# Head norms of an attention stage: sums of squares from two rounded parts instead of one float32 product

## What is computed

```python
def rms_norm(x, g):
    xf = x.astype(jnp.float32)
    y = xf * lax.rsqrt(jnp.mean(xf * xf, axis=-1, keepdims=True) + EPS)
    return (y * g.astype(jnp.float32)).astype(x.dtype)

q, k, v, g, fl = jnp.split(proj, ...)          # 16 heads of 64
q = rms_norm(hd(q), qnorm_g).transpose(0, 2, 1, 3)
k = rms_norm(hd(k), knorm_g).transpose(0, 2, 1, 3)
for blk in range(s_ // FOX_BLOCK):             # 4 blocks of 128 queries
    logits = q[block] @ k[:q1].T * scale + cumf[:, None] - cumf[None, :]
    probs = softmax(where(mask, logits, -inf))
    outs.append(probs @ v[:, :, :q1])
o = o * jax.nn.silu(g)
```

## Time and profile before

| | |
|---|---|
| median of three runs | 2725.76 us |
| the profiled execution | 2727.36 us |
| its span in the trace | 2725.9 us |
| mean granted TensorE clock | 0.996 of full |
| TensorE busy | 2663.0 us, 98% |
| VectorE busy | 1941.1 us, 71% |
| ScalarE busy | 1064.7 us, 39% |
| GpSimd busy | 575.8 us, 21% |

### The profile page before, as it was taken

How to read it: one execution, slowest core, us unless ns; L and a number is a source line. 1 busy time by engine, 2 the same in 40 slices (tenths; PEclk the granted TensorE clock), 3 DMA queues, 4 the chain that set the end, 5 groups by cost and what they waited for, 6 DMA issues and landing times.

```text
span 2725.9 us, 38343 instructions
## 1 busy us (share of the span) xinstructions
PE 2663.0 (98%) x15829; PEld 2294.1 (84%) x15829; DVE 1941.1 (71%) x2645; ACT 1064.7 (39%) x1512; POOL 575.8 (21%) x366
## 2 busy tenths in 40 slices
PE   9899999999999999999999999999999999999998
PEld 6687877678899988878899988999978778788997
DVE  7888644656888865458888788888744743888887
ACT  4444555543443325443333424433322222343342
POOL 2211000101444300002444214443000000044440
PEclk9999999999999999999999999999999999999999
DMA  9453222222333232222333323333423213233331
GB/s 299 143 152 113 62 62 62 78 62 78 109 93 109 94 109 86 70 62 78 109 111 106 109 78 109 96 106 95 134 81 105 86 63 99 62 109 94 97 120 47
DMA packets 297457, 268.31 MB, mean 98 GB/s; under 512 B 10999, under 2 KB 265217, under 8 KB 297026
## 3 DMA queue, kind: packets, MB, share of 16 engines
q1 hardware_dynamic: 294050, 256.99, 30.6%
q0 software_dynamic: 2368, 6.64, 0.7%
q10 hardware_dynamic: 864, 2.23, 0.3%
HBM read 263.72 MB, written 2.10 MB: 98 GB/s over the span
## 4 chain that ended last, share of the span: by engine, by line
PE 76%; DVE 16%; ACT 3%; issue 3%; POOL 1%; DMA 1%; SPq 0%; DVEq 0%; ACTq 0%; POOLq 0%
PE psum L355 13%; PE psum L357 13%; PE psum L356 13%; PE psum L434 6%; PE psum L435 6%; PE psum L436 6%; PE psum L411 2%; PE psum L413 2%; PE psum L412 2%; DVE acc L530 2%; DVE w_lo L340 1%; PE psum L3409 1%; DVE w_lo L1043 1%; DVE stat L679 1%; PE psum L2953 1%
## 5 line engine op out<-in xcount | busy, mean ns | idle before, releaser
L355 PE MATMUL psum<-h_hi,w_hi 128*128 128x256 f32 (+1 forms) x2224 | 721.7, 325 | 18.5 <-DVE f_cffn L1063 6.5
L357 PE MATMUL psum<-h_hi,w_lo 128*128 128x256 f32 (+1 forms) x2224 | 702.8, 316 | 0.0
L356 PE MATMUL psum<-h_lo,w_hi 128*128 128x256 f32 (+1 forms) x2224 | 701.9, 316 | 0.0
L355 PEld LDWEIGHTS psum<-h_hi,w_hi 128*128 128x128 f32 x2224 | 426.0, 192 | 54.0 <-issue 12.7
L356 PEld LDWEIGHTS psum<-h_lo,w_hi 128*128 128x128 f32 x2224 | 426.3, 192 | 29.0 <-issue 5.5
L357 PEld LDWEIGHTS psum<-h_hi,w_lo 128*128 128x128 f32 x2224 | 425.8, 191 | 27.1
L989 POOL TENSOR_TENSOR val<-w_raw 128x512 f32<-128x512 f32 x72 | 100.2, 1392 | 1355.6 <-DMA w_raw<-in_ffn_w_in 954.8
L340 DVE TENSOR_TENSOR w_lo<-w_raw,w_hi 128x2048 fp32r<-128x2048 f32 x98 | 223.4, 2291 | 150.3 <-ACT w_hi L335 140.7
L530 DVE SCALAR_TENSOR_TENSOR acc<-psum,acc 128x512 f32<-128x512 f32 x416 | 269.8, 679 | 42.0 <-PE psum L436 42.0
L355 PE MATMUL psum<-t_hiffn,w_hi 128*128 128x256 f32 x864 | 245.2, 284 | 3.4 <-DVE w_lo L1043 2.3
L356 PE MATMUL psum<-t_loffn,w_hi 128*128 128x256 f32 x864 | 244.5, 283 | 0.0
(11 more groups left out here) (442 smaller groups left out, 5479.9 us busy)
## 6 DMA issues: line engine op xcount, KB each, us to landing
w_raw<-in_ffn_w_in SPq DMA_DIRECT2D x176, 512.0 KB, 5.1
w_raw<-in_ffn_w_out SPq DMA_DIRECT2D x88, 512.0 KB, 6.3
w_raw<-in_ret_w_in SPq DMA_DIRECT2D x48, 512.0 KB, 4.7
ada_raw<-in_ada_w SPq DMA_DIRECT2D x32, 512.0 KB, 4.7
w_raw<-in_odd_w_in SPq DMA_DIRECT2D x32, 512.0 KB, 5.0
w_raw<-in_even_w_in SPq DMA_DIRECT2D x24, 512.0 KB, 6.7
w_raw<-in_gla_w_in SPq DMA_DIRECT2D x24, 512.0 KB, 4.9
ada_first<-in_ada_w SPq DMA_DIRECT2D x32, 256.0 KB, 6.3
```

What stands on the lines that cost most here:

```text
L355: k.nc.tensor.matmul(out, ws, xs, start=first, stop=False)
L356: k.nc.tensor.matmul(out, ws, xl, start=False, stop=False)
L357: return k.nc.tensor.matmul(out, wl, xs, start=False, stop=last)
```

## The change

Each square is made in two float32r parts. ScalarE's square (L2488) writes a rounded `o_sq_hi`. GpSimd makes the exact square from the copied tile and subtracts the rounded one, giving `o_sq_lo`. TensorE multiplies both by a float32r block of ones, so one float32 product becomes two float32r products. In the fills the sum stands two steps later (`m == 5`); the output fill's place is unchanged. At the stage's start the sums move too: k 0 0 from behind `tensor_narrow` to the second step of v, q 0 1 from step 4 to step 6 of v's first half, k 0 1 from step 1 to step 3 of its second half. VectorE's norm also waits for `o_sq_lo`, since it overwrites the copied tile. GpSimd's gates stand between and behind the squares. `o_g` moves into the constants `reset128` and `reset64`, to make room.

```diff
-                if m == 3 and normed:
+                if m == 5 and normed:
                     tensor_head_norm(k, *normed, 7)
...
-    pe.matmul(k.bank[b][:], k.const("block_ones"), k.o_sq, start=True, stop=True
-              ).then_inc(*k.up("o_sum", (w, i, c)))
+    pe.wait_ge(*k.at("o_sq_lo", (w, i, c)))
+    pe.matmul(k.bank[b][:], k.o_ones[:], k.o_sq_hi[:], start=True, stop=False)
+    pe.matmul(k.bank[b][:], k.o_ones[:], k.o_sq_lo[:], start=False, stop=True).then_inc(*k.up("o_sum", (w, i, c)))
...
-    sc.activation(k.o_sq, k.bank[b][:], ACT.Square).then_inc(*k.up("o_sq", (w, i, c)))
+    sc.activation(k.o_sq_hi[:], k.bank[b][:], ACT.Square).then_inc(*k.up("o_sq", (w, i, c)))
+
+
+def gpsimd_square(k, w, i, c):
+
+    po, before = k.nc.gpsimd, norm_before(w, i, c)
+    raw = (k.o_qn if w == "q" else k.o_kn)[:, c, :]
+    po.wait_ge(*k.at("o_raw", (w, i, c)))
+    if before:
+        po.wait_ge(*k.at("o_sq_lo", before))
+    po.tensor_tensor(k.o_sq, raw, raw, MULT).then_inc(*k.pool.up())
+    po.wait_ge(*k.pool.at())
+    po.wait_ge(*k.at("o_sq", (w, i, c)))
+    po.tensor_tensor(k.o_sq_lo[:], k.o_sq, k.o_sq_hi[:].bitcast(F32), SUB).then_inc(*k.up("o_sq_lo", (w, i, c)))
...
     ve.wait_ge(*k.at("o_rs", (w, i, c)))
+    ve.wait_ge(*k.at("o_sq_lo", (w, i, c)))
...
     tensor_narrow(k, S, 2)
-    tensor_head_norm(k, "k", 0, 0, 3)
     pe.wait_ge(*k.at("w_lo", n_v))
-    for x, norms in enumerate(({4: ("q", 0, 1)}, {1: ("k", 0, 1)})):
+    for x, norms in enumerate(({1: ("k", 0, 0), 6: ("q", 0, 1)}, {3: ("k", 0, 1)})):
...
+    sc.activation(k.o_ones[:], k.const("block_ones"), ACT.Copy)
     sc.wait_ge(*k.at("used", AT[S, "q", 0]))
...
 def gpsimd_odd(k):
-    for i in range(4):
-        gpsimd_gate(k, AT["odd", "out", i])
+    for x, (w, i, c) in enumerate(NORMS):
+        gpsimd_square(k, w, i, c)
+        if x == 9:
+            gpsimd_gate(k, AT["odd", "out", 0])
+        if x == 11:
+            gpsimd_gate(k, AT["odd", "out", 1])
+    gpsimd_gate(k, AT["odd", "out", 2])
+    gpsimd_gate(k, AT["odd", "out", 3])
```

More of the change, by code:

```diff
@@ L186 @@
 SAME = ("cross", "cross_copied", "diag", "keep", "out", "values", "cum", "ex", "E", "edge", "q", "sq", "sum",
-        "v_copied", "silu", "S", "turned", "scores", "norm", "half")
+        "v_copied", "silu", "S", "d", "turned", "scores", "norm", "half")
 def signal(name):
@@ L2772, in scalar_fill @@
             sc.wait_ge(*k.at("o_g_raw", (i, 1)))
-            sc.activation(k.o_g[:], k.o_g[:], ACT.Silu).then_inc(*k.up("o_silu", i))
+            sc.activation(k.o_g, k.o_g, ACT.Silu).then_inc(*k.up("o_silu", i))
             sc.preload_act_table_set(EXP_LN)
@@ L3629, in tiles @@
             k.gq8 = sb("o_gq8", [P, 1], ctx=c2)
-            k.o_qn, k.o_kn, k.o_g = (sb(n, [P, 2, T], ctx=c2) for n in ("o_qn", "o_kn", "o_g"))
+            k.o_qn, k.o_kn = (sb(n, [P, 2, T], ctx=c2) for n in ("o_qn", "o_kn"))
+            k.o_g = k.const("reset128", 0, 2 * T).rearrange("p (a n) -> p a n", n=T)
+            k.o_sq_hi, k.o_sq_lo = (sb(n, [P, T], F32R, c2) for n in ("o_sq_hi", "o_sq_lo"))
+            k.o_ones = sb("o_ones", [P, P], F32R, c2)
             k.o_v = [sb(n, [P, NT, 256], ctx=c2) for n in ("o_v0", "o_v1")]
```

## The result

| | before | after |
|---|---|---|
| median of 19 runs each, same comparison | 2726.26 us | 2729.83 us |
| ratio, 95% interval | | 1.0014, [1.0008, 1.002] |
| the profiled execution | 2727.36 us | 2733.22 us |
| its span | 2725.9 us | 2731.7 us |
| mean granted TensorE clock | 0.996 | 0.995 |

The change made the kernel slower by 3.6 us, 0.14%. The interval doesn't contain 1, so the slowing is measured; its amount lies within the 0.2% that the prediction called the same. One of the 19 runs before took 6913.14 us, and the ratio leaves it out. The forecast was +7.6.

What follows compares the result with a forecast made beforehand. The prediction took the stage to be PE's program laid end to end. Its terms, +3.2 - 0.2 + 0.8 + 3.8, gave +7.6 us (6.2 saved against 13.8 in waits), a median of 2733.4 us, range 2725.0 to 2738.

Steps and rivals of the forecast that it cites:

- the likeliest case: Whole kernel: waits outweigh the saved products, +7.6 us, time 2731.3 to 2737; chance 0.52.
- few collisions: Rival: DVE's pairs go through together, POOL's operations fall into DVE's idle time; -0.8 to +5 us, 2725 to 2731; chance 0.35.
- the wait for turned part 4: Product with v, slots 0, 1, 2, 3 and 5: ACT's turned part 4 stands behind the root; 0.6 us each.
- The product: Each norm's sum: two float32r products cost 0.47 us against 0.855 for float32; 0.385 saved, 6.2 us over 16 norms.
- GpSimd's part: From the copy's end to `o_sq_lo`: product and difference take 2.6 us, 2.7 with hand-overs.
- Start: Stage start until the scores of tile 1 in slot 0: waits and DVE collisions, 0.6 to 3.9 us later, taken as +3.2.
- all with them: Upper end at the stage's start: scores of tile 1 start at 353.6 with all collisions, 350.3 without.
- Slots 0 to 4: Eight norms save 3.1 us, turned part 4 costs 2.4, gate 0 costs 0.5: -0.2; slot 4 nothing.
- Slot 5: Late low part, scalings of tile 3 held by POOL and the wait for turned part 4: +0.8 us; -0.7 without collisions.
- Slot 6: Gates 2 and 3 behind k 3 1's difference hold both scalings of tile 0; scores of tile 2 wait 3.8 us.
- As dear as float32: Rival: a float32r pair costs as much as the float32 product, 6.2 us not saved, about 2739; chance 0.05.
- Faster: Rival: products count and waits at the start fill later slack, -5.5 to -6.8 us, 2719 to 2720; chance 0.08.

Runs made afterwards that it cites:

- GpSimd's part made, but not waited for: Kernel after with sums at the old places reading the rounded square twice, nothing on PE or DVE waiting for the low part: 2726.07 us, ratio 0.9997.
- the gates alone: Kernel without GpSimd squares (two products of the rounded square, old places), with each gate put behind the square where the change put it: 2721.43 us, ratio 0.998.
- the third gate moved: Kernel after with the gate of output piece 2 put in front of the square of q 3 1, in slot 5: 2728.16 us, ratio 1.0006.
- the start in float32: Kernel after with the first four norms as in the kernel before (float32 product, no GpSimd square, old places): 2727.93 us, ratio 1.0005.
- the products alone: Kernel after without GpSimd squares, both float32r products reading the rounded square, sums and gates as in the kernel before: 2720.02 us, ratio 0.9976.
- the version with these two mended, and the start left in float32: Kernel after with the first four norms in float32, sums behind the fifth step (sixth in slot 5), gate 2 in slot 5: 2722.13 us, ratio 0.9987.
- the three parts: Separate kernels' effects on the stage: products exchanged -6.0 us, sums' places moved +2.7, GpSimd's work beside VectorE without being waited for +6.1.

## Why the prediction was right and wrong

The range held the time, and the sign of the likeliest case was right. The size was not: +7.6 was forecast, 3.6 came, and the time fell into the 2725 to 2731 of the case called few collisions. I had given 0.35 to within 0.2% and 0.57 to slower by more. The mechanisms of the likeliest case were all there, though: the wait for turned part 4, waits on GpSimd at the start, DVE operations held by gates in slot 6. It was their prices in PE's time that were too high, always in the same direction. So the sign and the range were earned, but the 2729.83 itself was that of a case which I had held to be the less likely.

**The product: right.** 0.385 a norm was forecast, 0.40 came at the places that the earlier trace rows shows, 6.0 us in all when alone.

**GpSimd's part: right, a little long.** 2.6 us was forecast for both operations; 1.04 and 1.28 came. Whether the product is shorter for its one input or for being a product, no run here tells. POOL's busy time rose by 44.5 us, against 42, but 16 norms of 2.32 are 37: the rest is for the most part time in which DVE held GpSimd's operations, which the working had only at the stage's start.

**Start: +3.2 forecast, +1.96 measured.** The wait at the sum of q 0 1 was right: 2.0 to 3.5 forecast, 3.07 came, and the order by which it was worked out (scan, product, k's norm, difference) is nearly that of the trace; only the norm came ahead of the product and not behind it. The step that failed is the last one, "all with them". The wait at k 0 1 was 0.98 and not 1.1 to 1.6, and then nothing was late at the scores of tile 1: PE is there at 354.41 without a wait. DVE was late, its maximum of tile 0 by 3.2 us on the stage's own scale (352.80 against 346.81 us, less the 2.78). But before the change the exponentials behind that maximum were done 1.4 us before PE asked for them (DVE's reciprocal, which waits for them, begins at 348.30, the scores of tile 1 at 349.67), and now PE itself came 2 us later: 0.1 us of slack was left (354.30 against 354.41). 3.07 + 0.98, less four savings of 0.40 and the 0.6 of the earlier trace rows that went, is 1.85. So PE's waits and DVE's delays ran side by side, and this term was the waits on PE alone; DVE's delays alone, with no wait for the low part, cost 3.0 us here (GpSimd's part made, but not waited for). I had put the second behind the first.

**Slots 0 to 4: -0.2 forecast, -0.40 measured.** The wait for turned part 4 was forecast at 0.6 and came at 0.64, five times. The fourth fill's sum took its 0.3 to 0.5 of slack and no more, as forecast. Gate 0 met a scaling, as forecast (456.37 to 460.10 us), and cost PE nothing: the 0.5 put on it was the part that missed. In the kernel with the gates alone the same gate met the negation instead, and there it cost the half microsecond.

**Slot 5: +0.8 forecast, -0.56 measured,** k 3 1's saving in both. The wait for q 3 0's low part was 0.57 against 0.9, and turn 0 waited 0.74 where it was forecast to be 1.3 late. The scalings of tile 3 did have GpSimd's product between them, but it held the second one for 0.8 us (1.66 for the pair against 0.88 in the earlier trace rows), not for a whole product of 1.3. And a wait that was there before became shorter: that for the exponentials before the scores of tile 2 fell from 0.94 to 0.28, since the gate of piece 1 began 0.25 us behind the pair of scalings and let it through. With the third gate moved it began 0.06 behind them, and the wait was 0.9 again, as it was with the start in float32. That part, 0.66 of the 1.4 us by which this term missed, is chance: nothing in the change sets where that gate falls to a fifth of a microsecond, since it starts when its piece is loaded.

**Slot 6: +3.8 forecast, 2.2 measured,** 1.51 and 0.56 in waits. Right: both gates in one row behind k 3 1's difference, two DVE instructions held for almost a gate each. Wrong: which ones. The forecast had both scalings of a pair; the first gate held a negation of 128x2 numbers, which I had not counted as an operation that a gate could hold. And k 3 1's difference ended 2.8 us behind the product with v and not 3.65, so the gate began 0.86 us ahead of the negation (557.05 against 557.91); by the forecast's time it would have begun beside it. That moved the wait from tile 2 to tile 1 and made two small ones of it, and what both hold up overlaps. PE's own arrival was put at 11.7 us on that scale, where the earlier trace rows give 12.27 less 0.385, so 11.9; that slip is 0.2 of the 1.6.

The four terms sum to +3.2 against +7.6, and the misses are 1.2, 0.2, 1.4 and 1.6. Two of the large ones, the start and slot 6, are of one kind: DVE's delays were carried through to PE without the slack between the two, or laid end to end with a delay that ran beside them. The third, slot 5, is half chance. The clock is a price that the prediction put at nothing without a word: at the wait of 3.07 us it fell to 0.50 in two of the three profiles that have this wait, for 0.8 us net, and not in the profile after. The earlier trace rows gave DVE 20 idle us of 31 in a slot, and I used this for the rival only.

What was to be seen if each step held was there: the spacing of 0.23, some 42 us more of POOL, five idle times of 0.6 at the product with v, 2 to 3.5 at the sum of q 0 1. Only the last sign, two scalings of over 4 us in slot 6 and 3.8 in front of tile 2, came in another form.

**The rivals.** "As dear as float32" is ruled out by the products alone. "Faster" was wrong for the change, and right for its parts: it decides where I had put it, at the wait for turned part 4 and at the gates, and the version with these two mended, and the start left in float32, is 3.5 to 4.2 us faster than before. The ports: the Trainium skill ("SBUF — State Buffer", section "SBUF: two separate sides") has the lock for DVE's two-port modes as well as for two SBUF inputs; the cast (0.41 to 1.41) and the 128x2 negation (0.17 to 3.76) bear that out, neither of which has two tiles as input. Maxima, which read PSUM (0.42 at 557.45 us, with a gate under way), were not held. Nor was the reciprocal of 128x2, from SBUF to SBUF (0.17 at 562.55, with a gate under way), so where the operands lie is not enough to tell. My own sentence that the two take turns one instruction at a time was too simple: at 338.25 us DVE had two in a row while GpSimd waited.

**What stays open.** The 6.1 us of GpSimd's work are split by place; by operation only slot 6 is, where the squares alone cost nothing, the gates' places alone 0.76 and both 2.2 to 2.8. How often the clock falls at the wait of 3.07 us in runs without a profile is open too: the mean clock of the kernel after is that of the kernel before, 0.996. Whether the sizes of the three parts hold in the whole is shown only by their sum, which is 0.4 to 0.8 us short of it.

## What to carry to other kernels

Before work goes to GpSimd, list the VectorE instructions beside it that a trace shows held, the tiny ones too, and follow each delay through to TensorE's next wait rather than adding it up: here 2.3 us of work a norm cost 6 us in all, with neither TensorE nor VectorE waiting for its result, at the start and in slot 6 for nearly all of it. When a step of a fixed order is moved, set its place for each slot by what is in front of it on the engine that feeds it and behind it on the engine that follows; one number for all slots was wrong at 3 and at 5. When a kernel is slower by more than its waits, look at the clock before looking for another wait. And count a saving on the bounding engine and its price apart, by two kernels, before both are put into one: -6.0, +2.7 and +6.1 told more here than their sum of about 3.

## What the runs showed of the hardware

- A DVE instruction of 128x2 elements, SBUF to SBUF, was held for 3.76 us by a gate on GpSimd of 4.6; alone it takes 0.17. Being small protects nothing.
- Not all such instructions are held: the reciprocal, 128x2 and SBUF to SBUF too, took 0.17 us at 562.55 with a gate under way from 561.6, and a maximum that reads PSUM 0.42 at 557.45.
- Whether a gate of 4.6 us holds a pair of scalings or lets it through was decided by less than 0.2 us: begun 0.25 behind the pair's start it let both through (0.48), begun 0.06 behind it, or 0.12 in the kernel before, it held one (4.81).
- A cast of 16x512 from float32 to bf16 took 1.15 to 1.41 us beside GpSimd and 0.41 without.
- GpSimd is held as well: its product, 1.04 us otherwise, took 2.37 behind a scan and the norm that followed, and 2.89 from 451.00 us on, where a weight piece of 2.28 had begun on DVE at 450.70. The scan itself took 1.22 both times.
- GpSimd's product of a tile with itself took 1.04 us, the difference of two tiles 1.27 to 1.29, both for 128x512 in float32.
- The granted TensorE clock fell to 0.50 for 3.4 us at the end of an idle time of 3.07 us in two profiles (from 340.2 and from 337.3 us) and stayed at 1.00 behind the same idle time in a third. Products of 128x256 started 0.21 us apart while it was 0.50, and 0.12 apart at 1.00.
